# Rows of the products' moving operands 32 bytes further apart in SBUF

## What is computed

```python
# first block
proj  = rmsnorm(h) @ w_in                 # linear-attention and sparse-attention mixers on it
h     = h + mixed @ w_out
q     = rmsnorm(h) @ wq                   # product keys: top 16 of 128 x 128 experts, 8 heads
act   = gelu(u[expert] . x);  h += sum(w * act * v[expert])
h     = h + (p @ ple_proj) * sigmoid(rmsnorm(h) @ ple_gate_w)
# two layers: neighbourhood attention, grouped-query attention, each followed by
h     = h + gate * (attention(ada_norm(h) @ w_qkv) @ w_o)
h     = h + gate * ((silu(a) * b) @ ffn_w_out),   a, b = split(ada_norm(h) @ ffn_w_in)
```

## Time and profile before

| | |
|---|---|
| median of 3 runs | 2177.85 us (2175.31 to 2178.85) |
| the profiled execution | 2176.95 us |
| its span, first to last instruction | 2175.2 us |
| TensorE busy (PE) | 2073.0 us, 95% |
| weight loads (PEld), beside it | 1828.1 us, 84% |
| VectorE busy | 1253.0 us, 58% |
| ScalarE busy | 1036.3 us, 48% |
| mean DMA rate | 151 GB/s |
| mean granted TensorE clock | 0.981 of full speed |

### The profile page before, as it was taken

One profiled execution on the slowest core, in us unless ns is written; L12 is line 12 of the kernel. 1 busy time (PEld: TensorE's weight loads), 2 busy tenths in 40 slices (PEclk: granted clock), 3 DMA queues, 4 the chain that ended last, 5 costly groups with the idle time before them and its releaser, 6 DMA issues. The chain is left out here.

```text
span 2175.2 us, 36150 instructions
## 1 busy us (share of the span) xinstructions
PE 2073.0 (95%) x15028; PEld 1828.1 (84%) x15028; DVE 1253.0 (58%) x1939; ACT 1036.3 (48%) x1896; POOL 33.4 (2%) x32
## 2 busy tenths in 40 slices
PE   7988999999998999999998999989999998999998
PEld 6858989999998999999986876768888887679998
DVE  6776588877887555555574237553333225556554
ACT  5664444467776444444464226443232215555543
POOL 0000000000000000000010000010000001000000
PEclk9989999999999999999998999999999999999999
DMA  6603577754444777777754310122223232114553
GB/s 209 200 1 126 175 261 261 260 177 146 146 141 132 237 265 260 254 260 259 243 175 165 96 59 2 59 78 88 96 88 101 93 97 90 53 41 163 186 190 120
DMA packets 91250, 329.15 MB, mean 151 GB/s; under 512 B 10064, under 2 KB 12496, under 8 KB 90832
## 3 DMA queue, kind: packets, MB, share of 16 engines
q1 hardware_dynamic: 91088, 326.85, 45.4%
HBM read 325.76 MB, written 1.05 MB: 150 GB/s over the span
## 5 line engine op out<-in xcount | busy, mean ns | idle before, releaser
L321 DVE TENSOR_TENSOR wlo<-raw,whi 128x1024 fp32r<-128x1024 f32 (+1 forms) x502 | 614.5, 1226 | 567.5 <-ACT whi L315 564.6
L315 ACT ACTIVATE whi<-raw 128x1024 fp32r<-128x1024 f32 (+1 forms) x502 | 527.0, 1052 | 472.7 <-PE ps L503 428.4
L501 PE MATMUL ps<-x_hi,whi 128*128 128x512 f32 (+1 forms) x1040 | 360.5, 347 | 28.3 <-DVE x_lo L484 23.2
L502 PE MATMUL ps<-x_lo,whi 128*128 128x512 f32 (+1 forms) x1040 | 358.4, 345 | 0.0
L503 PE MATMUL ps<-x_hi,wlo 128*128 128x512 f32 (+1 forms) x1040 | 358.2, 344 | 0.0
L501 PE MATMUL ps<-xT_hi,whi 128*128 128x256 f32 x1152 | 329.6, 286 | 4.1 <-DVE xT_lo L482 4.1
L502 PE MATMUL ps<-xT_lo,whi 128*128 128x256 f32 x1152 | 322.3, 280 | 0.0
L503 PE MATMUL ps<-xT_hi,wlo 128*128 128x256 f32 x1152 | 321.9, 279 | 0.0
L501 PE MATMUL ps<-gh,whi 128*128 128x256 f32 x1024 | 290.4, 284 | 5.6 <-DVE gl L1813 5.6
L502 PE MATMUL ps<-gl,whi 128*128 128x256 f32 x1024 | 286.9, 280 | 0.0
L503 PE MATMUL ps<-gh,wlo 128*128 128x256 f32 x1024 | 286.7, 280 | 0.0
(11 more groups left out here) (354 smaller groups left out, 2965.8 us busy)
## 6 DMA issues: line engine op xcount, KB each, us to landing
raw<-peer_u_t SPq DMA_DIRECT2D x128, 512.0 KB, 3.6
raw<-peer_v_t SPq DMA_DIRECT2D x128, 512.0 KB, 4.4
raw<-ada_t SPq DMA_DIRECT2D x96, 512.0 KB, 5.4
raw<-ffn_in_t SPq DMA_DIRECT2D x88, 512.0 KB, 3.5
raw<-ffn_out_t SPq DMA_DIRECT2D x44, 512.0 KB, 3.8
raw<-qkv_t SPq DMA_DIRECT2D x36, 512.0 KB, 3.5
raw<-w_in_t SPq DMA_DIRECT2D x24, 512.0 KB, 4.3
raw<-peer_wq_t SPq DMA_DIRECT2D x16, 512.0 KB, 3.5
```

Source lines behind the costliest of these rows:

```text
L315: act.activation(whi[:, n % SPLIT, 0:w], raw[:, g % RAW, 0:w], ACT.Copy).then_inc(hi_done, 1)
L321: dve.tensor_tensor(wlo[:, n % SPLIT, 0:w], raw[:, g % RAW, 0:w], whi[:, n % SPLIT, 0:w].bitcast(F32), ALU.subtract).then_inc(lo_done, 1)
L501: pe.matmul(place, wh, xh, start=start, stop=False, skip_group_check=shared)
L502: pe.matmul(place, wh, xl, start=False, stop=False, skip_group_check=shared)
```

## The change

A helper allocates the buffer with rows that are eight float32 values (32 bytes) longer, and gives back the view without them. It is used for `aT`, `xT`, `gh`/`gl`, `x2`, `xg` and, in the feed-forward, for `hid` where it is 256 columns wide (the second layer); in the first layer `hid` stays as it was. `pT`, `whi` and `wlo` stay too. No instruction is added, removed or moved, on any engine or queue, and the tensors that are placed behind a spaced one move up by a multiple of 32 bytes.

```diff
+        SPACE = 8
+
+        def spaced(stack, name, rows, n):
+
+            x = stack.enter_context(nc.sbuf_tensor(name, [P, rows, n + SPACE], F32R))
+            return x[:, :, 0:n]
+
...
-        aH = [mixer.enter_context(nc.sbuf_tensor(n, [P, C, T], F32R)) for n in ("aT_hi", "aT_lo")]
+        aH = [spaced(mixer, n, C, T) for n in ("aT_hi", "aT_lo")]
...
-        ffn_norm.parts = xH = [pb(n, [P, C, T], F32R) for n in ("xT_hi", "xT_lo")]
+        ffn_norm.parts = xH = [spaced(keys_space, n, C, T) for n in ("xT_hi", "xT_lo")]
...
-            gh = own.enter_context(nc.sbuf_tensor("gh", [P, 3, T], F32R))
-            gl = own.enter_context(nc.sbuf_tensor("gl", [P, 3, T], F32R))
+            gh, gl = (spaced(own, n, 3, T) for n in ("gh", "gl"))
...
-        x2H = [ctx.enter_context(nc.sbuf_tensor(n, [P, C, TT], F32R)) for n in ("x2_hi", "x2_lo")]
+        x2H = [spaced(ctx, n, C, TT) for n in ("x2_hi", "x2_lo")]
...
-            xgH = [ob(n, [P, C, T], F32R) for n in ("xg_hi", "xg_lo")]
+            xgH = [spaced(own, n, C, T) for n in ("xg_hi", "xg_lo")]
...
-                hid = [own.enter_context(nc.sbuf_tensor(f"ffn_{n}{i}", [P, FC, w], F32R)) for n in ("hi", "lo")]
+                hid = [spaced(own, f"ffn_{n}{i}", FC, w) if w == T else own.enter_context(nc.sbuf_tensor(f"ffn_{n}{i}", [P, FC, w], F32R)) for n in ("hi", "lo")]
```

## The result

The changed kernel takes 2190.55 us (median of 4 runs, 2187.19 to 2192.10) where the kernel before took 2177.80 beside it: 12.75 us more, a ratio of 1.0058 with a 95% interval of 1.0041 to 1.0076. The interval lies above 1. All ratios of this document leave out one run of the kernel with rows 128 bytes further apart, which took 2774.91 us at a mean granted clock of 0.695; all others had 0.976 to 0.984. The forecast was no change; rival A, slower through the place of the rows, is what happened.

A forecast was written before the change was run, and what follows sets the result against it. The prediction took TensorE to bound the kernel, busy for 2073.0 of 2175.2 us. Its terms, moving operand, weights, ScalarE and VectorE writes and moved buffers, summed to 0, so the forecast was the median, 2178 us, range 2165 to 2204.

The forecast's parts named there:

- rival A: 256-column matmuls: where a row begins relative to the weights matters, 12 to 19 us slower, 2190 to 2197 us; chance 0.28.
- The likeliest case: Whole kernel: the time stays the same, 2178 us, reaching from 2174 to 2182; chance 0.55.
- Part (a): Spaced rows as moving operand of 9360 256-column and 1680 512-column matmuls: taken as 0, between -8.4 and +30.9 us.
- The price is of each column: Key stage and first feed-forward: 116.7 and 233.3 ns give 0.456 ns per column and only 0.1 ns fixed per matmul.
- `xg` has the alignment of `xT` and differs: `xg` matmuls: 117.8 ns, 1.1 over, at the alignment of `xT`, so alignment does not, or not alone, tell cases apart.
- The 280-column rows: 280-column tiles: second row, at 96 modulo 128, takes 126.7 ns against the first's 128, so no dearer, rather 0.9 cheaper.
- the equal 512-column time with weights moving: 512 columns with split weights moving, row at 0 modulo 128: 234 ns, read as the same as 233.3.
- Parts (b) to (d): Spaced rows as weights, ScalarE and VectorE writing spaced rows, and buffers behind moving by multiples of 32 bytes: each costs nothing.
- (b): Spaced rows as weights in 384 products: loads stay hidden and cost nothing; some 28 us at most if not.
- point of decision: Key and value loops: slower through row place is decided once the mean distance exceeds 117.2 ns, 4.7 us over 9360 matmuls.
- Rivals B and C: B: differently beginning rows meet less often, 2170 to 2174 us, 0.08. C: per-column time is a row clash, 2068, 0.09.
- The rule weighed in the prediction: SBUF reads pay per crossing into a new 16-byte line; starts at multiples of 32 bytes keep the crossings, so no change.

## Why the prediction was right or wrong

The measured 2190.55 us lies in the stated range of 2165 to 2204 only because the range took in rival A, which had a chance of 0.28. The likeliest case, no change at 0.55, missed by 12.6 us.

**What bounds the kernel** was right: TensorE. 14.2 us more of its busy time came with 15.1 us more of the span.

**Part (a), the moving operand, is the step that failed.** It took 0 between bounds of -8.4 and +30.9 us; measured are +12.0 by the gauges and 12.75 in the medians. The upper bound was the right reading of the right row: `pT`'s 120.0 ns is what every stage shows when all rows lie at its place against the weights, and that run's span was 27.7 us longer than before. Three arguments led away from it.

- "The price is of each column, so nothing fixed is there to change" rested on 116.7 and 233.3 being in proportion. They are, at place 32. At place 0 the pair is 120.0 and 226.6, which by the same sum makes 0.416 ns a column and 13.4 ns a matmul. Two widths at one place don't give a law.
- "`xg` has the alignment of `xT` and differs, so alignment is not what tells". `xg` has two rates at the very same place, 117.8 ns before and 116.7 with two buffers spaced. An exception was taken as a refutation.
- The 280-column rows and the equal 512-column time with weights moving were read as evidence that starts don't count. Measured against the stationary row, the tile's two rows lie at places 224 and 64, not at 0 and 96, and at 256 columns 64 is also the slightly cheaper of these two (117.7 for 118.4 ns). At 512 columns five of the seven places seen do give 233.4; the two that don't were not among those in the trace.

**Parts (b) to (d)** hold in size. ScalarE and VectorE have the same busy times to 1.2 us, and everything moved by 32 bytes leaves the gauge as it was. In (b) the place of a spaced row as the weights counts as well (229.1 ns for 234 in the tall tile above), but its matmuls are few.

**Rival A** had the mechanism and the size, 12 to 19 us for 12.75, and its point of decision: a mean above 117.2 ns, measured 118.2. In part that is luck, since three details were off. It counted places modulo 128; they count modulo 256. It gave each place a quarter of the matmuls, which `gh` and `gl` with three rows do not have. And it said that 512-column products would stay; they became 1.2 ns shorter. The quarter it could not see, at 64, is 117.7 at one of its two places and 113.4 at the other when all rows lie there. **Rivals B and C** did not occur. C's 0.421 ns a column was not reached: the shortest distance at 512 columns, 226.6 ns, is 0.443 ns a column. What the record has of the sum of squares is 216 ns between starts at 256 columns; that each passes its columns twice is the prediction's reading.

The rule weighed in the prediction, from the Trainium skill ("SBUF — State Buffer", section "Door 1: The DMA port swizzle", on 16-byte lines), gave no change. It does not explain the trace: places that are all multiples of 32 bytes differ by up to 6.6 ns.

## What to carry to other kernels

Where TensorE is the bound with `float32r` operands, the distance between starts of a steady stream is a thing to compare between stages with the addresses beside it: a small group that is 3% slower, as `pT` was, can be a measurement of what others would be at its place. One group is not enough to settle it, since the same place showed two rates in some stages. The change of layout that spread rows over many places came out near the mean of them, so such a change helps only if the present place is worse than the mean. Read the rate at several places by one cheap shift of the buffers before spacing anything, and at every width that the kernel uses, for the best place differs by width.

## What the runs showed of the hardware

In this kernel a `float32r` matmul's distance to the next depends on the start of its moving operand against that of its stationary one, modulo 256 bytes: 113.4 to 120.0 ns at 256 columns, 226.6 to 233.4 at 512, with the clock granted in full. Moving both together by 32 bytes changed nothing. A stretch can keep its rate for tens of microseconds, but a place can have two: 113.4 and 118.0 ns at 192, 116.7 and 117.8 at 32, 113.5 and 117.7 at 64, and 229.0 and 233.3 at 64 with 512 columns. Where the place changes every three matmuls, single rows depart from the table by up to 3.5 ns. That two reads of TensorE get into each other's way, the moving row's and the next weights', would fit the dependence on relative place and is argued, not shown: no run took the weight loads away.
